# Six reordered places and a split of the layer-norm sums in a three-layer transformer kernel on one core

## The reference, cut to what matters

```python
# layer 0: modulation from c, sparse-indexer attention (8 heads) and a short convolution, then SwiGLU
mod = silu(c) @ w_ada + b_ada                       # six vectors: sh1, sc1, g1, sh2, sc2, g2
mix = token_mixer(x * (1 + sc1) + sh1, ...)         # attention over 64 chosen keys, conv, two group norms, @ w_out
x = layer_norm(2**0.25 * x + g1 * mix, ln1_g, ln1_b)
x = layer_norm(2**0.25 * x + g2 * swiglu(x * (1 + sc2) + sh2, ...), ln2_g, ln2_b)
# layer 1 and 2: a mixer, a SwiGLU, and a gated addition of a projected side input p
x = x + gla_mixer(rms_norm(x, norm_mix[0]), ...)    # gated linear attention, 4 heads, both directions
x = x + swiglu_2(rms_norm(x, norm_ffn[0]), ...)     # width 2816
x = x + sigmoid(rms_norm(x, ple_norm[0]) @ w_gate) * (p[0] @ w_proj)
x = x + diff_attn_mixer(rms_norm(x, norm_mix[1]), ...)   # 8 heads, two softmaxes and their difference
...                                                 # and the SwiGLU and the gated addition again
def layer_norm(x, g, b):
    mu = mean(x); var = mean(square(x - mu))
    return (x - mu) * rsqrt(var + 1e-5) * g + b
```

## Time and profile before

| | |
|---|---|
| median of 3 runs | 1086.41 us (1084.53 to 1087.03) |
| the profiled execution, its own time | 1086.66 us |
| its span in the trace | 1084.9 us |
| TensorE busy | 1045.9 us, 96% of the span |
| VectorE busy | 731.6 us, 67% |
| ScalarE busy | 553.1 us, 51% |
| GpSimd busy | 207.5 us, 19% |
| mean granted TensorE clock | 0.991 of full speed |
| DMA, mean over the span | 178 GB/s |

### The profile page before, as it was taken

How to read it: one execution, slowest core, us unless ns; L and a number is a source line. 1 busy time by engine, 2 the same in 40 slices (tenths; PEclk the granted TensorE clock), 3 DMA queues, 4 the chain that set the end, 5 groups by cost and what they waited for, 6 DMA issues and landing times.

```text
span 1084.9 us, 20420 instructions
## 1 busy us (share of the span) xinstructions
PE 1045.9 (96%) x7985; PEld 983.2 (91%) x7985; DVE 731.6 (67%) x1155; ACT 553.1 (51%) x946; POOL 207.5 (19%) x227
## 2 busy tenths in 40 slices
PE   5999998999999999999999999999998999999998
PEld 5677787999999988989999999998976999999998
DVE  5697767676745786768656655686787766564565
ACT  2223466544554594527645443566566764454443
POOL 0000013323321101013233320121210223332010
PEclk9999999999999989999999999999999999999999
DMA  9993452577656544602655456663330464644661
GB/s 351 400 373 125 155 195 78 175 240 260 208 155 185 165 155 155 215 20 91 220 187 200 133 153 179 243 223 134 123 133 3 154 233 157 219 141 128 193 208 40
DMA packets 183587, 192.78 MB, mean 178 GB/s; under 512 B 5913, under 2 KB 143426, under 8 KB 183522
## 3 DMA queue, kind: packets, MB, share of 16 engines
q1 hardware_dynamic: 182512, 191.15, 52.0%
q0 software_dynamic: 144, 0.52, 0.2%
q10 hardware_dynamic: 866, 0.21, 0.1%
HBM read 190.83 MB, written 1.05 MB: 177 GB/s over the span
## 4 chain that ended last, share of the span: by engine, by line
PE 56%; DVE 5%; ACT 3%; issue 1%; POOL 0%; DVEq 0%; POOLq 0%; ACTq 0%
PE gemm L2205 16%; PE gemm L2207 16%; PE gemm L2206 16%; DVE wlo L1461 1%; PE aux L2693 1%; ACT whi L897 1%; PE aux L2813 1%; PE aux L2743 1%; PE aux L2205 1%; DVE prod L1935 1%; PE aux L2207 1%; PE aux L2206 1%; PE gemm L2796 0%; PE aux L2749 0%; DVE state L2061 0%
## 5 line engine op out<-in xcount | busy, mean ns | idle before, releaser
L1461 DVE TENSOR_TENSOR wlo<-raw,whi 128x1024 fp32r<-128x1024 f32 (+1 forms) x308 | 353.4, 1191 | 62.5 <-ACT whi L897 61.8
L2205 PE MATMUL gemm<-ohi,whi 128*128 128x256 f32 x1376 | 389.1, 283 | 3.7 <-issue 1.1
L2206 PE MATMUL gemm<-olo,whi 128*128 128x256 f32 x1376 | 386.6, 281 | 0.0
L2207 PE MATMUL gemm<-ohi,wlo 128*128 128x256 f32 x1376 | 384.7, 280 | 0.0
L897 ACT ACTIVATE whi<-raw 128x1024 fp32r<-128x1024 f32 (+1 forms) x308 | 276.5, 963 | 59.6 <-PE gemm L2207 47.5
L2205 PEld LDWEIGHTS gemm<-ohi,whi 128*128 128x128 f32 x1376 | 259.8, 189 | 7.3 <-issue 3.2
L2206 PEld LDWEIGHTS gemm<-olo,whi 128*128 128x128 f32 x1376 | 259.9, 189 | 0.6 <-issue 0.5
L2207 PEld LDWEIGHTS gemm<-ohi,wlo 128*128 128x128 f32 x1376 | 259.9, 189 | 0.0
L2207 PE MATMUL gemm<-acthi,wlo 128*128 128x256 f32 x528 | 147.7, 280 | 0.0
L2205 PE MATMUL gemm<-acthi,whi 128*128 128x256 f32 x528 | 147.7, 280 | 0.0
L2206 PE MATMUL gemm<-actlo,whi 128*128 128x256 f32 x528 | 147.3, 279 | 0.0
(11 more groups left out here) (379 smaller groups left out, 1558.1 us busy)
## 6 DMA issues: line engine op xcount, KB each, us to landing
raw<-in_ffn_w_in SPq DMA_DIRECT2D x44, 1024.0 KB, 6.7
raw<-in_ffn_w_out SPq DMA_DIRECT2D x32, 704.0 KB, 5.3
part<-in_w_ada SPq DMA_DIRECT2D x32, 512.0 KB, 9.5
raw<-in_gla_w_in SPq DMA_DIRECT2D x6, 2048.0 KB, 8.4
raw<-in_diff_w_in SPq DMA_DIRECT2D x6, 2048.0 KB, 8.0
raw<-in_w_gate SPq DMA_DIRECT2D x11, 1024.0 KB, 6.3
raw<-in_w_up SPq DMA_DIRECT2D x11, 1024.0 KB, 8.5
raw<-in_w_down SPq DMA_DIRECT2D x16, 704.0 KB, 5.5
```

The lines of the kernel that those rows point to most:

```text
L1461: dve.tensor_tensor(wlo[hslot][:, q * w:(q + 1) * w], src[:, q * w:(q + 1) * w], whi[hslot][:, q * w:(q + 1) * w].bitcast(F32), ALU.subtra ...
L2205: pe.matmul(dst, st_hi, mv_hi, start=start, stop=False)
L2206: pe.matmul(dst, st_hi, mv_lo, start=False, stop=False)
L2207: return pe.matmul(dst, st_lo, mv_hi, start=False, stop=stop_)
```

## The change

Seven edits, all of them about what stands where; the arithmetic of the layer norms is shared out differently, and nothing else is computed in another way.

1. In the heads of layer 0, DVE takes the maxima of head 0 before the low parts of `out0`; two of these four quarters move into heads 1 and 2. ACT takes the squares of group 2 ahead of a quarter of `out0`.
2. In `out0`'s second block the last low quarter for `gate_up0` moves behind output tile 3.
3. In both layer norms POOL adds tiles 0 to 5 only. PE multiplies tile 6 and its square by ones itself: two more products in each layer norm.
4. At the start of the linear attention DVE copies one part of the side projection, adds the squares, copies the next, makes `z_lo`, and copies the first two parts only after the gate inputs (`pp_late`). PE does the sums and z behind the third tile of `gla_q`, ahead of the last two steps of the fourth.
5. In `gla_v` all four quarters stand at tile 0, and the exponentials are shared out over both blocks.
6. In the differential attention the quarters of `out2` stand beside heads 1 to 4 on ACT (before: 3, 4, 5 and 7) and 2 to 5 on DVE (before: 4, 5, 6 and 8).
7. At the tail of that attention PE does both last transpositions, then the sums of group 1, then both value products; the sums of group 2 move into the first step of `out2`. ACT and DVE follow.

```diff
@@ ACT and DVE: which quarters stand beside which tile @@
-            if first and ph.name in WIDE:
+            if first and ph.name in WIDE or ph.name == "gla_v":
                 each = (4, 0, 0, 0)
...
+            if ph.name == "out0" and not act:
+                return {0: (1,), 1: (2,), 3: (3,)}.get(t, ())
@@ POOL, layer_sums @@
-                for t in range(1, KT - 1):
+                for t in range(1, KT - 2):
...
-                    me.did(ins, sums_ready if t == KT - 2 else None)
+                    me.did(ins, sums_ready if t == KT - 3 else None)
@@ ACT, beside_head @@
+                if i == 6:
+                    group_squares(2, gated_ready, 2)
                 if i in (5, 6):
                     split(PH["out0"], At(1), i - 5)
                 if i == 6:
-                    group_squares(2, gated_ready, 2)
                     high_parts(0, 1)
@@ ACT, gla_after @@
-                if at.i == 0 and t == 1:
-                    for d in range(2):
+                if (at.i, t) in ((0, 1), (1, 0)):
+                    for d in (at.i,):
@@ ACT, heads of the differential attention @@
+                if i == 7:
+                    pair_root(0, X[1])
+                    squares((1,), d_o, d_nsq)
...
-                if 3 <= i <= 5 or i == 7:
-                    ahead(*OUT2, min(i - 3, 3))
-                if i == 7:
-                    pair_root(0, X[1])
-                    squares((1,), d_o, d_nsq)
+                if 1 <= i <= 4:
+                    ahead(*OUT2, i - 1)
             wait(act, tile_done, PH["diff_v"].tile0 + 4)
             high_parts_of(0, 1)
+            pair_root(1, X[1])
             squares((2,), d_o, d_nsq)
-            pair_root(1, X[1])
@@ DVE, heads of layer 0 @@
-            for q in range(4):
+            masked_maxima(0)
+            for q in range(2):
                 low(PH["out0"], At(0), q)
             modulate_part(10)
-            masked_maxima(0)
...
+                if i in (1, 2):
+                    low(PH["out0"], At(0), i + 1)
@@ DVE, start of the linear attention (take_projection(n) copies bank n of the projection) @@
+            take_projection(2, pp_ready[0])
             SQUARED = 4
             for t in range(1, KT):
                 dve.wait_ge(sq_ready, SQUARED + t + 1)
                 me.link(dve.tensor_tensor(sq_sum[:, :], ...))
+            take_projection(3, pp_ready[0])
+            dve.wait_ge(z_hi_ready, 1)
+            dve.tensor_tensor(z_lo[:, :], ...)
...
+            for n in range(2):
+                take_projection(n, pp_late)
@@ DVE, heads of the differential attention @@
-                if i == NH + 1:
+                if i == NH:
                     wait(dve, tile_done, PH["diff_v"].tile0 + 4)
                     make_pair(0)
-                if i == NH + 2:
+                if i == NH + 1:
                     low_pair(0)
...
-                if 4 <= i <= 6 or i == 8:
-                    low(*OUT2, min(i - 4, 3))
+                if 2 <= i <= 5:
+                    low(*OUT2, i - 2)
@@ PE, first_sums @@
+                pe.wait_ge(dve_read, STREAM[0] + KT - 1)
+                pe.matmul(X[0][:, 0:T], ones[:, :], tl(res, KT - 2), start=True, stop=False)
+                pe.wait_ge(ln_sq_ready, me.n.get(ln_sq_ready.name, 0) + KT - 1)
+                pe.matmul(X[1][:, 0:T], ones[:, :], tl(ln_sq, KT - 2), start=True, stop=False)
                 me.next(sums_ready)
@@ PE, gla_q: stats, z and its wait run as after(at, t) at t == 2 @@
-            gemm("gla_q", dve_read, olo_from=start)
+            gemm("gla_q", dve_read, olo_from=start, after=sums_and_gates)
@@ PE, heads of the differential attention @@
+                if 2 <= i < NH:
+                    attend(i - 2)
                 if i < NH:
                     value_steps(16 + 6 * i, 22 + 6 * i)
+                if 1 <= i <= NH:
+                    transposes(i - 1)
                 if i in (6, 8):
                     group_stats((i // 2 - 3,), ones[:, :], d_nsq, X[1:2])
...
+                if i >= NH:
+                    attend(i - 2)
-            group_stats((2,), ones[:, :], d_nsq, X[0:1])
             start = next_operand()
             gemm("out2", dve_read, olo_from=start, operand=(xhi, xlo),
-                 beside={1: lambda: group_stats((3,), ones[:, :], d_nsq, X[1:2])})
+                 beside={0: lambda: group_stats((2,), ones[:, :], d_nsq, X[0:1]),
+                         1: lambda: group_stats((3,), ones[:, :], d_nsq, X[1:2])})
```

More of the change, by code:

```diff
@@ L1959, in _, with take_projection @@
             layer_norm(1)
[L1960 removed]
+            def take_projection(n, ready):
                 dve.wait_ge(pp_done, n + 1)
[L1962 removed]
+                for dst, bank in dict(pp_copies(1))[n]:
                     ins = dve.tensor_copy(dst, bank)
[L1964 to L1967 removed]
+                ins.then_inc(ready, 1)
+            take_projection(2, pp_ready[0])
             SQUARED = 4
@@ L2538, in projection_of @@
                     if t % 2 == 0:
-                        banks.claim(bank, pp_ready[n])
+                        banks.claim(bank, pp_late if (n, t < 4) == (0, True) else pp_ready[n])
                     for k in range(2):
@@ L2635, in _, with sums_and_gates @@
             start = next_operand()
-            gemm("gla_q", dve_read, olo_from=start)
-            stats(tok=True, summed=gla_summed)
-            pe.wait_ge(z_lo_ready, 1)
-            banks.claim(X[1], z_ready)
-            for k in range(KT):
-                ins = three(X[1][0:48, 0:T], z_hi[:, 48 * k:48 * (k + 1)], z_lo[:, 48 * k:48 * (k + 1)], tl(ohi, k),
-                            tl(olo, k), k == 0, k == KT - 1)
-            ins.then_inc(z_done, 1)
+            def sums_and_gates(at, t):
+                if t != 2:
+                    return
+                stats(tok=True, summed=gla_summed)
+                pe.wait_ge(z_lo_ready, 1)
+                banks.claim(X[1], z_ready)
+                for k in range(KT):
+                    ins = three(X[1][0:48, 0:T], z_hi[:, 48 * k:48 * (k + 1)], z_lo[:, 48 * k:48 * (k + 1)], tl(ohi, k),
+                                tl(olo, k), k == 0, k == KT - 1)
+                ins.then_inc(z_done, 1)
+            gemm("gla_q", dve_read, olo_from=start, after=sums_and_gates)
             pe.wait_ge(z_ready, 1)
@@ L2802, in _, with attend, transposes @@
             scores(0)
+            def attend(h):
+                banks.claim(X[2], mixed_ready)
+                me.next(pt_ready)
+                if h % 2 == 0:
+                    pe.wait_ge(v_ready, 4 + h // 2 + 1)
+                for kt in range(2):
+                    ins = pe.matmul(X[2][:, 0:T], d_v[:, kt * D + h * P:kt * D + (h + 1) * P],
+                                    tl(d_pt, h % 2, w=512)[:, kt * T:(kt + 1) * T], start=(kt == 0), stop=(kt == 1))
+                ins.then_inc(pv_done, 1)
+            def transposes(h):
+                s = h % 2
+                banks.claim(X[0], pt_ready)
+                me.next(prob_ready)
+                for kt in range(2):
+                    for qt in range(2):
+                        ins = pe.transpose(X[0][:, kt * T + qt * P:kt * T + (qt + 1) * P],
+                                           tl(d_p, 4 * s + qt)[:, kt * P:(kt + 1) * P], ident)
+                ins.then_inc(trans_done, 1)
             for i in range(NH + 2):
```

40 lines of the change are left out of this document (10 added, 30 removed).

## The result

The changed kernel takes 1079.13 us (median of 6 runs, 1077.75 to 1081.72), the kernel before 1086.42 us in the same comparison. The ratio is 0.9931, 95% interval 0.9915 to 0.9948: faster by 0.7%. The forecast was 1079.3 us. The profiled execution took 1077.96 us, so the two traces lie 8.7 us apart, 1.4 us more than the medians.

A forecast was written before the change was run, and what follows sets the result against it. TensorE was taken as the bound, busy 1045.9 of 1084.9 us. The terms summed to -7.1 us from the profiled 1086.66, so 1079.6, and 1079.3 us as the median lies 0.25 lower; range 1075.0 to 1085.0 us.

The forecast's parts named there:

- A: Heads of layer 0: maxima of head 0 no longer wait, but VectorE's work is only moved; -0.5 us.
- B: Squares ahead of the quarter of `out0`: they come 0.95 us sooner, with 0.3 us of new wait at head 7; -0.6 us.
- C: First layer norm: wait for GpSimd's sums goes (-2.0), two products added (+0.86), slow clock avoided (-1.7); -2.9 us.
- D: Second layer norm: two added products cost 0.86 us and cover the 0.47 us wait for tile 7; +0.4 us.
- E: Start of the linear attention: squares added sooner, waits shrink, `gla_k`'s last low part comes behind two copies; -0.9 us.
- F: `gla_v`: the four low parts end over 1.8 us earlier, removing the 0.83 us wait; -0.8 us.
- G: Differential attention: 3.7 us won at the tail, less one new 1.9 us wait at head 4's scores; -1.8 us.

The follow-up runs named there:

- experiment 1: The changed kernel with only VectorE's order in the heads of layer 0 put back: 1079.8 us, ratio 0.9943 to the kernel before.
- experiment 2: The changed kernel with only the layer-norm sums put back on GpSimd (tiles 0 to 6): 1079.5 us, ratio 0.9952 to the kernel before.
- experiment 5: The changed kernel with VectorE's last low quarter for `gate_up0` put back behind output tile 2 of `out0`: 1078.82 us, ratio 0.9924 to the kernel before.
- experiment 6: The kernel before with only the shared-out layer-norm sums (GpSimd adds tiles 0 to 5, TensorE multiplies tile 6 and its square): 1084.28 us, ratio 0.9968.
- experiment 9: The changed kernel without the edits to the linear attention's start, `gla_v` and the differential attention's tail: 1082.56 us, ratio 0.9951 to the kernel before.
- experiment 3: The changed kernel with layer-norm sums back on GpSimd and four filler products ahead of TensorE's wait in each layer norm: 1084.17 us, ratio 0.9982 to the kernel before.

## Why the prediction was right

**A, right in mechanism, and in sign and size only with the clock's help.** VectorE's work was only moved: waits of 0.7, 0.9, 0.6 and 1.3 us stand for one of 2.4. But the prediction kept two slow stretches and passed over a third that stood behind a place of the change: behind the 2.4 us wait TensorE ran at 1.2 GHz for 3.4 us (6.8 us in experiment 1), and with the new order it mostly does not. Against an old order without that stretch the edit would by the estimate in experiment 1 lose a microsecond.

```profile
89.60:93.00 3.40, 3.40 (x9) 2.31 (x9) 1.45 (x5) 2.61 (x10) 0.00 (x0) 0.50 1.05 407
```

**B, right, size and mechanism.** -0.63 for -0.6: the products behind the squares come 0.94 us sooner, and the new wait for the inverted sums of head 7 is the 0.3 us that was estimated. No run puts this edit back by itself; this is read from the two traces.

**C, right in size; the mechanism was half the story.** The prediction gave the gain to the shared-out sums and left 0.4 us, at its lower bound, to the moved low part. Experiments 2, 5 and 6 show two edits of which either removes the most: 2.36 us by edit 2, 2.87 us by edit 3, the slow stretch in both. I had seen GpSimd's additions of 1.5 us and more in the trace, but had read the lateness as a matter of how many additions there are.

Of the clock, the prediction's sentence on the skill said that the 1.7 us could be luck. All eleven traces with edit 2 or edit 3 are at full clock behind this layer norm; in the one without both TensorE waits 1.84 us there, and the clock falls. One trace is no proof that it always does, so how much of the 1.7 us is the order's in the long run stays open. Two things speak for the order: full clock in eleven of eleven, and the mean granted clock of all executions, 0.990 in 43 of the kernel before and 0.992 in ten with edit 3 alone (0.987 to 0.997), where one stretch of 3.4 us less would make 0.0016. The rule of the Trainium skill (TensorE: Matmul & The Clock Gate, Part 1: The HAM clock gate) that the place of the change shifts from run to run isn't seen behind this layer norm once the wait is gone. At `gla_k` it fits: of the traces with edit 4 as it stands in the change, four have a stretch of 3.4 us there and three one of 6.8.

**D, over-sized.** +0.11 for +0.4: start to start the covered wait was worth 0.75 us (0.86 - 0.11), not 0.47.

**E, right in mechanism, in size by luck.** The prediction let the last low part set the start of `gla_k`, at 397.1 where the gates alone would have allowed 396.6, so 0.5 us behind them; the gates came 1.4 us sooner instead of 1.1, and the wait is 0.94 us. For the edit it took -0.9 and -0.92 was measured, but experiment 9 gives only 0.5 us to the edit itself and 0.4 to the clock: the term was mis-sized by 0.4 us, and the clock made it good. The further 1.15 us behind `gla_k` are clock too: about 6 us of the 100 matmuls were at 1.2 GHz before, 3.4 us in this trace.

**F, right.** -0.94 for -0.8, and experiment 9 brings the wait back.

**G, every mechanism right, the sum off by 1.3 us.** The scores of head 4 come 1.94 us later than before, for 1.9, and one head pays it, not four. The tail gave 4.05 us for 3.7. What failed is the step "I take one such wait: -3.7 + 1.9", which priced the wait and nothing behind it: the clock fell there and doubled the products of 3.4 us, 1.6 us more. The prediction had found the wait; that it would cost a slow stretch was nowhere in the sum.

**The sum.** -7.1 was forecast and the medians say -7.3. The profiled executions differ by 8.7 because 1.4 us lie ahead of everything that changed: the twelve profiles reach the scores of head 0 between 84.6 and 86.5 us whichever order they have (84.64 in experiment 1, 86.45 in experiment 2). With the 1.15 us at `gla_k` that is 2.5 us of chance on the good side, and the slow stretch in G is 1.6 us against it. So the forecast of 1079.3 hit 1079.13 within 0.2 us by luck as well; the terms of the sum are good to 0.4 us each, and G to 1.3, and those of A, C and E hold some 1.6, 1.7 and 0.4 us of clock, of which C's rests on one trace.

## What to carry to other kernels

A wait taken away on the bottleneck engine shows its worth only after the engine that was waited for has been followed through the next steps: four of the seven places (A, B, E and G) paid part of the gain back as a new wait, and each could be read from the trace before. An early split of a weight block that waits for the last reader of its buffer holds up all that stands behind it; moved one head later it cost nothing and was worth about half as much as the whole change. When two edits aim at one wait, run each alone before either gets the credit. And when a wait has a slow stretch behind it, price the stretch beside the wait, for waits that go and for waits that come.

## What the runs showed of the hardware

**GpSimd and VectorE side by side.** GpSimd's addition of 128x256 takes 0.73 us when VectorE isn't at a low part of 128x1024, and 1.53 to 1.73 us when VectorE is already at one; a low part takes 1.22 us, and 1.3 to 1.75 us when an addition is already running. Two meetings in the first layer norm, from experiments 6 and 2:

```profile
167.59 1.23 DVE L1461 TENSOR_TENSOR wlo<-raw,whi 128x1024 fp32r<-128x1024 f32 x1
167.89 1.53 POOL L818 TENSOR_TENSOR mean<-mean,res 128x256 f32<-128x256 f32 x1
169.38 0.73 POOL L820 TENSOR_TENSOR sq_sum<-sq_sum,ln_sq 128x256 f32<-128x256 f32 x1
...
169.04 0.72 POOL L822 TENSOR_TENSOR sq_sum<-sq_sum,ln_sq 128x256 f32<-128x256 f32 x1
169.22 1.63 DVE L1464 TENSOR_TENSOR wlo<-raw,whi 128x1024 fp32r<-128x1024 f32 x1
```

In the first the low part starts first and keeps its 1.23 us, and the addition takes twice its time; the next addition meets nothing. In the second the addition starts first and keeps its 0.72, and the low part takes 1.63. The Trainium skill (SBUF — State Buffer, SBUF: two separate sides) says that a VectorE operation with two inputs in SBUF and one of GpSimd take turns at a port pair that they share, and that the later one is blocked. The traces agree: of two that meet, the later one gets longer and the earlier one doesn't.

**Slow stretches.** In every trace those that end before the kernel does are 3.4 or 6.8 us long at 1.2 GHz. The stretch in the differential attention is there in six of the eight traces that have the 1.9 us wait (not in experiments 3 and 9), and in none of the four without it. In the heads of layer 0 it is there in all three traces with a wait of 2.3 us and more, and in one of nine with a wait of 0.7. Ahead of the first layer norm's sums a wait of 1.84 us had one behind it, a wait of 1.13 us (experiment 2) had none. Such a wait makes the stretch likely and not certain. What decides it stays open.

**A scatter without a known cause.** The feed-forward part of layer 0, the same instructions in all twelve traces, took 188.8 us in seven of them and 189.9 us in five (before, changed, 3, 6 and 9). No wait in it differs, and the clock is full in all: matmuls start 116.7 ns apart on average in the seven and 117.8 ns in the five, evenly over some 125 us. An effect of a microsecond can't be read across such a part, which is why the places were read by landmarks close to them.
